# A hybrid decoder layer on Trainium2: gated-unit columns ahead of the decay projection, vectors fetched by another queue

## The chip, the core and the metric

The kernel runs on one core of one Trainium2 chip. The metric is device time in microseconds of one execution. The engines of the core are TensorE (PE: matmuls and transposes, results in PSUM), VectorE (DVE), ScalarE (ACT: activations, some with tables of functions that have to be loaded), GpSimd (POOL) and SyncE (SP, which only issues DMAs here). ScalarE can issue DMAs too, on a queue of its own. Engines wait for each other through semaphores: `then_inc` counts one up when an instruction is done, `wait_ge` holds the engine until a count is reached. A DMA counts 16.

## What is computed

A decoder layer on 256 tokens of width 1024 in float32: RMS norm, one projection that feeds forgetting attention (8 heads) and a gated convolution of width 31, an output projection, a second RMS norm, a top-4-of-32 mixture of experts and a final norm. Cut to the part that the change touches:

```
xn = rmsnorm(h, norm_mix_g);  proj = xn @ w_in
q, k, v, f_logit, glu_in = split(proj);  glu_in = glu_in + b_glu
log_f = log_sigmoid(f_logit + b_f)            # (8 heads, 256)
c = cumsum(log_f)                             # s[t, j] = q_t.k_j * scale + c_t - c_j, causal
a, g = split(glu_in);  u = a * sigmoid(g)     # (256, 512)
y = depthwise_conv(u, w_dw, width 31, causal) + b_dw
conv_o = silu(layernorm(y, ln_g, ln_b))
h = h + concat(att_o, conv_o) @ w_out
h = h + moe(rmsnorm(h, norm_ffn_g))           # 32 experts, 12 MB of weights each
```

## The kernel before

Every engine's program is written out by hand, in order. All big weights stream from HBM into a ring of 22 units of 1 MB in SBUF (`ring`), issued by SyncE: first the pieces of `w_in` and `w_out`, then the experts' weights through L422. On the first lap the ring's places are still in use as pieces and scratch, so SyncE waits for `released_slots` before it writes one: the places of the gated unit's weights for `proj_done` 5, of q for 7, of k for 9, of v for 11, and later ones for scores, for parts of the output projection, and so on. From the second lap on it waits for `units_used`, which TensorE counts.

The first 137 us are the layer before the experts. ScalarE issues two DMAs (decay weights `wf_sb` and `bf_col`, L549, L550), loads a table, and then, for each of the two tiles of 128 tokens, squares and sums x (L553) and takes the root (L562); VectorE does the mean, the reciprocal and the scaling (L801, L803, L823). SyncE issues x (L367), then six small vectors (norm gains, biases, L370 and L372), the taps (L373), then the four quarters of the gated unit's weights (L378). TensorE turns the vectors into columns (L1193, L1195; semaphore `vecs_turned`), ScalarE copies them to `cols`, TensorE transposes the normalised tiles (L1189), VectorE scales them by the gain into `xn_t` (L828) and ScalarE does one of the four groups (L568).

TensorE then runs, in this order: the decay projection into four partial sums (8 matmuls, semaphore `f_done`), the transposes of the taps (L1221), and for each of four blocks of 128 channels the columns `a` (8 matmuls) and `g` (8 matmuls) of the gated unit, with the matmul that adds the four partial sums of the decay (`add_f_parts`) between `a` and `g` of block 0. Then come q and k (two passes each), part of v, the attention scores of groups 0 and 1, more of v, and the channel mean of the convolution's layer norm, for which it waits for `tap_done` (the convolution's channel sum).

ScalarE copies the decay's partial sums (L579) and logits (L587), and takes Exp (L589) and Ln (L591) of them, with VectorE steps between (L834 to L844), and only then goes through the blocks: sigmoid of `g` and a copy of `a` with bias (L597, L599), and, once VectorE has multiplied them (L854, `glu(c)`), taps 0 and 1 (L603, L605). VectorE adds the 29 other taps of each block one by one (L875, `tap_done`), into two accumulators by turns, with the next block's product in the middle, and at block 3, five taps before its end, the row maximum of score group 0 (`row_max(0)`, L862), which waits for `scores_done`. L1163 is the line of the helper that all matmuls share.

## Time and profile before

| | us |
|---|---|
| three timed runs | 1044.59, 1046.27, 1046.94 (median 1046.27) |
| profiled execution, its own time | 1044.2 |
| its span, first to last instruction | 1042.5 |
| PE busy in the span | 998.9 (96%) |
| DVE busy | 238.1 (23%) |
| ACT busy | 145.3 (14%) |
| mean granted TensorE clock | 0.990 |
| DMA, all queues | 421.75 MB, mean 405 GB/s |

The profile's page cuts the span into 40 equal slices of 26 us and gives what the DMA engines moved in each:

```profile
GB/s 310 393 414 194 220 367 395 425 416 427 426 427 436 428 430 427 434 426 432 428 435 428 431 429 431 432 429 429 435 426 431 428 432 429 429 433 424 426 425 167
```

The fourth and fifth slices, 78 to 130 us, are the low ones. In the rows further down a time is the start from the span's beginning, and "idle before <-releaser" is how long the engine had stood still and what let it go on. A TensorE matmul in float32 shows as two records, so 8 matmuls are x16.

### The profile page before, as it was taken

What the parts mean: (1) busy time and instruction counts of PE and PEld (TensorE: products, weight loads), DVE (VectorE), ACT (ScalarE), POOL (GpSimd) and SP (SyncE); (2) the same over time, 40 slices, a digit from 0 to 9 for tenths busy, and PEclk for the clock granted to TensorE, in tenths of its full rate; (3) what the DMA queues carried; (4) which work ended last, traced back from release to release, by engine and by line L of the source; (5) the groups of instructions that cost most, each with busy time, mean ns of one, the idle gap of its engine ahead of it and who ended that gap; (6) DMA issues with size and microseconds to landing.
All of it is one profiled execution on the core that took longest, in us unless ns stands there. A gap on an engine that the chain in (4) does not pass through costs nothing.

```text
span 1042.5 us, 12861 instructions
## 1 busy us (share of the span) xinstructions
PE 998.9 (96%) x5770; PEld 410.4 (39%) x5771; DVE 238.1 (23%) x532; ACT 145.3 (14%) x276; POOL 18.6 (2%) x29
## 2 busy tenths in 40 slices
PE   8999999999999999999999999989999999899996
PEld 7875534333333333333333333323333333323332
DVE  3995341111011111111111111101111111101121
ACT  5144320100010101010101001000101001000103
POOL 4000000000000000000000000000000000000001
PEclk9999999999999999999999999999999999999999
DMA  9995699999999999999999999999999999999994
GB/s 310 393 414 194 220 367 395 425 416 427 426 427 436 428 430 427 434 426 432 428 435 428 431 429 431 432 429 429 435 426 431 428 432 429 429 433 424 426 425 167
DMA packets 33381, 421.75 MB, mean 405 GB/s; under 512 B 4031, under 2 KB 8427, under 8 KB 14380
## 3 DMA queue, kind: packets, MB, share of 16 engines
q1 hardware_dynamic: 31772, 420.57, 96.0%
q8 instruction: 47, 0.77, 0.3%
q10 hardware_dynamic: 1552, 0.33, 0.2%
q14 instruction: 10, 0.08, 0.0%
HBM read 419.82 MB, written 1.05 MB: 404 GB/s over the span
## 4 chain that ended last, share of the span: by engine, by line
PE 61%; DMA 36%; DVE 1%; issue 1%; SPq 0%; ACT 0%; POOLq 0%; POOL 0%; DVEq 0%
PE work L1163 52%; DMA ring<-in_w_gu 32%; PE resid L1163 7%; DMA ring<-in_w_down 4%; PE work L1507 1%; DMA ring<-in_norm_ffn_g 0%; PE work L1279 0%; PE work L1470 0%; POOLq L148 0%; DVE main L929 0%; SPq L370 0%; POOL main L543 0%; PE work L1189 0%; DVE main L969 0%; DVE ring L828 0%
## 5 line engine op out<-in xcount | busy, mean ns | idle before, releaser
L1163 PE MATMUL work<-ring,main 128*64 128x512 f32 (+1 forms) x3080 | 684.8, 598 | 28.2 <-DMA ring<-in_w_gu 25.6
L1163 PEld LDWEIGHTS work<-ring,main 128*64 128x64 f32 (+1 forms) x3080 | 223.1, 139 | 471.3 <-issue 429.9
L1065 DVE TENSOR_SCALAR main<-work 128x512 f32<-128x512 f32 x32 | 22.1, 691 | 584.4 <-PE work L1163 584.4
L726 ACT ACTIVATE main<-main 128x512 f32<-128x512 f32 x32 | 20.2, 630 | 460.7 <-DVE main L1065 460.7
L1163 PE MATMUL work<-ring 128*128 128x256 f32 (+2 forms) x308 | 71.9, 403 | 1.8 <-DVE ring L828 0.9
L1163 PE MATMUL resid<-main 128*128 128x512 f32 x128 | 68.2, 618 | 0.9 <-DVE main L1134 0.9
L1163 PE MATMUL work<-bgu_rows,ident 128*64 128x512 f32 x256 | 62.2, 605 | 0.0
L1163 PEld LDWEIGHTS work<-ring 128*128 128x128 f32 (+1 forms) x308 | 55.7, 186 | 16.3 <-issue 8.3
L1163 PEld LDWEIGHTS work<-select,main 128*128 128x128 bf16 x1536 | 46.6, 98 | 26.2 <-issue 25.2
L740 ACT ACTIVATE main<-work 64x512 f32<-64x512 f32 x63 | 37.2, 591 | 117.9 <-PE work L1163 117.2
L1163 PE MATMUL work<-select,main 128*128 128x64 bf16 x1536 | 50.5, 194 | 0.1
L1058 DVE TENSOR_SCALAR lent<-count,place,gates 128x64 f32<-128x64 f32 x64 | 16.8, 306 | 146.9 <-PE work L1470 139.1
L875 DVE SCALAR_TENSOR_TENSOR main<-ring,main 128x256 f32<-128x256 f32 x116 | 46.6, 478 | 1.3 <-ACT main L605 1.2
L731 ACT ACTIVATE main<-work 128x512 f32<-128x512 f32 x32 | 19.1, 597 | 115.1 <-PE work L1507 115.1
L1072 DVE SCALAR_TENSOR_TENSOR main<-main 128x512 f32<-128x512 f32 x32 | 34.1, 1065 | 1.1
L1163 PEld LDWEIGHTS resid<-main 128*128 128x128 f32 x128 | 19.4, 190 | 27.4 <-issue 27.4
L1163 PE MATMUL resid<-ring,main 128*128 128x512 f32 (+1 forms) x68 | 28.8, 572 | 0.0
L1069 DVE TENSOR_TENSOR main<-main 128x512 f32<-128x512 f32 x32 | 22.2, 692 | 5.4 <-ACT main L726 5.4
L1163 PEld LDWEIGHTS work<-bgu_rows,ident 128*64 128x64 f32 x256 | 15.4, 135 | 19.4 <-issue 17.7
L1507 PEld LDWEIGHTS work<-ident,main 128*128 128x128 f32 x128 | 15.8, 141 | 17.9 <-issue 17.0
L737 ACT ACTIVATE main<-work 128x256 f32<-128x256 f32 x16 | 6.1, 383 | 114.7 <-PE work L1470 114.7
L1066 DVE TENSOR_SCALAR main<-work 128x512 f32<-128x512 f32 x32 | 21.8, 680 | 0.0
(188 smaller groups left out, 275.1 us busy)
## 6 DMA issues: line engine op xcount, KB each, us to landing
ring<-in_w_gu SPq DMA_DIRECT2D x36, 4096.0 KB, 41.6
ring<-in_w_gu SPq DMA_DIRECT2D x36, 2048.0 KB, 16.6
ring<-in_w_down SPq DMA_DIRECT2D x18, 4096.0 KB, 43.8
ring<-in_w_gu SPq DMA_DIRECT2D x8, 3072.0 KB, 37.5
ring<-in_w_down SPq DMA_DIRECT2D x11, 2048.0 KB, 15.6
ring<-in_w_down SPq DMA_DIRECT2D x20, 1024.0 KB, 14.2
ring<-in_w_gu SPq DMA_DIRECT2D x15, 1024.0 KB, 27.2
ring<-in_w_down SPq DMA_DIRECT2D x4, 3072.0 KB, 40.2
```

Of the source, the lines that this page charges most:

```text
L726: nc.scalar.activation(sig_h, gate_h, ACT.Sigmoid, scale=SWIGLU_ALPHA).then_inc(sig_ready, 1)
L731: nc.scalar.activation(to, work[:, act_bank(n), :], ACT.Copy).then_inc(act_t_ready, 1)
L737: nc.scalar.activation(scatter_sb[buffer][0:rows, :], work[0:rows, TURN_BANK, 0:TB * P], ACT.Copy).then_inc(scatter_ready, 1)
L740: return nc.scalar.activation(y_sb[buffer][h][parity * CAP:(parity + 1) * CAP, :], work[h * CAP:(h + 1) * CAP, bank, :], ACT.Copy)
L875: V.scalar_tensor_tensor(acc, u_pad[:, c, j:j + SEQ], dw_cols[:, c, j:j + 1], acc, ALU.mult, ALU.add)\
L1058: done = V.tensor_scalar(weighted[:, t, parity * CAP:(parity + 1) * CAP], count[:, bass.ds(r * CAP, CAP)], place[:, t, bass.ds(e, 1)], gat ...
L1065: V.tensor_scalar(gate_h, work[:, GATE_BANK, :], SWIGLU_LIMIT, None, ALU.min).then_inc(gate_clamped, 1)
L1066: V.tensor_scalar(up_h, work[:, UP_BANK, :], SWIGLU_LIMIT, -SWIGLU_LIMIT, ALU.min, ALU.max).then_inc(up_clamped, 1)
L1069: V.tensor_tensor(sig_h, sig_h, gate_h, ALU.mult).then_inc(glu_ready, 1)
L1072: V.scalar_tensor_tensor(gate_h.rearrange("p (b j) -> p j b", b=4), up_h.rearrange("p (j b) -> p j b", b=4), 1.0, sig_h.rearrange("p (j b) ...
L1163: return nc.tensor.matmul(out_, lhsT, rhs, start=start, stop=stop, skip_group_check=True)
L1507: last = nc.tensor.transpose(work[:, act_bank(n), j * P:(j + 1) * P], gate_h[:, j * P:(j + 1) * P], ident[:, :])
```

## The change

Four things are changed.

- The six small vectors are issued by ScalarE at the very start of its program, not by SyncE; the decay weights and `bf_col` are issued by ScalarE later, behind its copies of the transposed tile.
- ScalarE copies `cols` between the square and the root of the second tile, not behind both.
- TensorE's order is: transposes of the taps, columns of blocks 0 and 1, decay projection, `a` of block 2, the matmul that adds the decay's parts, `g` of block 2, then block 3 behind a wait for ScalarE's copy of the decay logits.
- ScalarE does block 0's activations first and the decay's Exp and Ln between the blocks; VectorE does the decay steps between the taps of block 1, at taps 5, 11 and 17, and the next block's product at tap 23 in blocks 0 and 1 (at 15 in block 2, as before).

```diff
@@ SyncE
             for t in range(TB):
                 sp.dma_start(x_sb[:, t, :], x[0, t * P:(t + 1) * P, :]).then_inc(x_in[t], 16)
-            at = 0
-            for vec, n in ((norm_mix_g, KB), (b_glu, 2 * CB), (b_dw, CB), (ln_g, CB), (ln_b, CB)):
-                sp.dma_start(vec_rows[at:at + n, :], vec.rearrange("(a p) -> a p", p=P)).then_inc(vecs_in, 16)
-                at += n
-            sp.dma_start(gain_rows, norm_ffn_g.rearrange("(m q) -> m q", q=4 * P)).then_inc(vecs_in, 16)
             sp.dma_start(dw_rows, w_dw).then_inc(dw_in, 16)
@@ ScalarE
-            act.wait_ge(wf_zeroed, 1)
-            act.dma_start(wf_sb[:, :, 0:HEADS], ...).then_inc(wf_in, 16)
-            act.dma_start(bf_col[:, :], ...).then_inc(bf_in, 16)
+            at = 0
+            for vec, n in ((norm_mix_g, KB), (b_glu, 2 * CB), (b_dw, CB), (ln_g, CB), (ln_b, CB)):
+                act.dma_start(vec_rows[at:at + n, :], vec.rearrange("(a p) -> a p", p=P)).then_inc(vecs_in, 16)
+                at += n
+            act.dma_start(gain_rows, norm_ffn_g.rearrange("(m q) -> m q", q=4 * P)).then_inc(vecs_in, 16)
...
                 mean_square(x_sb[:, t, :], xn[:, t, :], stat[:, t:t + 1], x_squared)
+                if t == TB - 1:
+                    act.wait_ge(vecs_turned, 1)
+                    nc.scalar.activation(cols[:, :], work[:, 3, 0:36], ACT.Copy).then_inc(cols_ready, 1)
                 act.wait_ge(x_mean, t + 1)
                 nc.scalar.activation(stat[:, 4 + t:5 + t], stat[:, 2 + t:3 + t], ACT.Sqrt).then_inc(x_root, 1)
-            act.wait_ge(vecs_turned, 1)
-            nc.scalar.activation(cols[:, :], work[:, 3, 0:36], ACT.Copy).then_inc(cols_ready, 1)
...
             done.then_inc(xnt_acted, 1)
+            act.wait_ge(wf_zeroed, 1)
+            act.dma_start(wf_sb[:, :, 0:HEADS], ...).then_inc(wf_in, 16)
+            act.dma_start(bf_col[:, :], ...).then_inc(bf_in, 16)
...
+            glu_halves(0)
+            first_taps(0)
+            glu_halves(1)
+            act.wait_ge(f_done, 1)
+            nc.scalar.activation(f_parts, work[:, 0, 0:SEQ], ACT.Copy).then_inc(f_copied, 1)
+            first_taps(1)
+            act.wait_ge(proj_done, F_SUM_DONE)
             act.wait_ge(bf_in, 16)
             nc.scalar.activation(fg[:, 0, :], work[0:HEADS, 0, 0:SEQ], ACT.Identity, bias=bf_col[:, :]).then_inc(proj_copied, 1)
             act.wait_ge(fg_step, 1)
             nc.scalar.activation(fg[:, 2, :], fg[:, 1, :], ACT.Exp).then_inc(decay_exp, 1)
             act.wait_ge(fg_step, 2)
             nc.scalar.activation(fg[:, 4, :], fg[:, 3, :], ACT.Ln).then_inc(decay_exp, 1)
+            for c in range(2, CB):
+                glu_halves(c)
+                first_taps(c)
@@ VectorE
+            NEXT_GLU = (TAPS - 8, TAPS - 8, TAPS // 2, None)
...
-                    if j == TAPS // 2 and c + 1 < CB:
+                    if j == NEXT_GLU[c]:
                         glu(c + 1)
+                    if (c, j) == (1, 5):
+                        decay_below()
+                    if (c, j) == (1, 11):
+                        decay_plus_one()
+                    if (c, j) == (1, 17):
+                        decay_sums()
                     if (c, j) == (CB - 1, TAPS - 6):
                         row_max(0)
@@ TensorE
+            for c in range(2):
+                glu_columns(c, "glu_a")
+                glu_columns(c, "glu_g").then_inc(proj_done, 1)
             pe.wait_ge(wf_in, 16)
             for kb in range(KB):
                 i = kb % 4
                 last = mm(work[32 * i:32 * i + 32, 0, 0:SEQ], wf_sb[:, kb, :], xn_t[:, kb, :], kb < 4, kb >= 4)
             last.then_inc(f_done, 1)
...
+            pe.wait_ge(cols_ready, 2)
+            glu_columns(2, "glu_a")
+            pe.wait_ge(f_sum_ready, 1)
+            pe.wait_ge(f_copied, 1)
+            mm(work[0:HEADS, 0, 0:SEQ], f_sum[:, :], f_parts, True, True).then_inc(proj_done, 1)
+            glu_columns(2, "glu_g").then_inc(proj_done, 1)
+            pe.wait_ge(proj_copied, F_SUM_DONE)
+            glu_columns(3, "glu_a")
+            glu_columns(3, "glu_g").then_inc(proj_done, 1)
```

What stands at three places before and after. First TensorE, from the transposes of the normalised tiles (128x128 x16) to the score matmuls; `32x256` is the decay projection, `128x31` the taps, `128x256` the columns, `8x256` the matmul that adds the decay's parts. Before:

```order
L1189 MATMUL work<-ident,ring 128x128 x16
L1163 MATMUL work<-ring 32x256 x8
L1221 MATMUL work<-ident,ring 128x31 x4
L1163 MATMUL work<-ring 128x256 x8
L1163 MATMUL work<-ring,lent 8x256
L1163 MATMUL work<-ring 128x256 x120
```

and after:

```order
L1209 MATMUL work<-ident,ring 128x128 x16
L1236 MATMUL work<-ident,ring 128x31 x4
L1183 MATMUL work<-ring 128x256 x32
L1183 MATMUL work<-ring 32x256 x8
L1183 MATMUL work<-ring 128x256 x8
L1183 MATMUL work<-ring,lent 8x256
L1183 MATMUL work<-ring 128x256 x88
```

The decay projection has moved behind 32 column matmuls and the adding matmul behind 40; the number of matmuls is the same.

Second ScalarE, from its first instruction to the root of the second tile (`DMA` is an issue). Before:

```order
L549 DMA ring<-in_w_in 128x8x8
L550 DMA bf_col<-in_b_f 8x1
L557 ACT_TABLE_LOAD
L557 ACTIVATE stat<-ident 128x1
L553 ACTIVATE ring,stat<-main 128x1024
L562 ACTIVATE stat<-stat 128x1
L553 ACTIVATE ring,stat<-main 128x1024
L562 ACTIVATE stat<-stat 128x1
L564 ACTIVATE cols<-work 128x36
```

and after:

```order
L546 DMA ring<-in_norm_mix_g 8x128
L546 DMA ring<-in_b_glu 8x128
L546 DMA ring<-in_b_dw 4x128
L546 DMA ring<-in_ln_g 4x128
L546 DMA ring<-in_ln_b 4x128
L548 DMA ring<-in_norm_ffn_g 2x512
L555 ACT_TABLE_LOAD
L555 ACTIVATE stat<-ident 128x1
L551 ACTIVATE ring,stat<-main 128x1024
L563 ACTIVATE stat<-stat 128x1
L551 ACTIVATE ring,stat<-main 128x1024
L561 ACTIVATE cols<-work 128x36
```

Six issues stand ahead of the table load where two stood, and the copy of `cols` stands ahead of the second root.

Third VectorE, in block 1 of the convolution (`128x256` of L875 or L889 is one tap, `8x256` a decay step). Before, the seven decay steps stood ahead of the first product:

```order
L834 SCALAR_TENSOR_TENSOR ring<-ring 8x256
L836 TENSOR_SCALAR ring<-ring 8x256
L838 SCALAR_TENSOR_TENSOR ring<-ring 8x256
L839 MEMSET ring 8x256
L841 SCALAR_TENSOR_TENSOR ring<-ring 8x256
L843 TENSOR_SCALAR ring<-ring 8x256
L844 TENSOR_SCALAR ring<-ring 8x256
L848 MEMSET ring 128x256
L854 TENSOR_TENSOR ring<-ring,main 128x256
```

and after, they stand between taps of block 1:

```order
L889 SCALAR_TENSOR_TENSOR main<-ring,main 128x256 x4
L845 SCALAR_TENSOR_TENSOR ring<-ring 8x256
L889 SCALAR_TENSOR_TENSOR main<-ring,main 128x256 x6
L849 TENSOR_SCALAR ring<-ring 8x256
L889 SCALAR_TENSOR_TENSOR main<-ring,main 128x256 x6
L853 SCALAR_TENSOR_TENSOR ring<-ring 8x256
L854 MEMSET ring 8x256
L856 SCALAR_TENSOR_TENSOR ring<-ring 8x256
L858 TENSOR_SCALAR ring<-ring 8x256
L859 TENSOR_SCALAR ring<-ring 8x256
L889 SCALAR_TENSOR_TENSOR main<-ring,main 128x256 x6
```

None is added or taken away; each of the three groups waits for ScalarE with taps queued behind it.

## Rows read from the trace of the kernel before

**Rows 1.** Stages: from:to, us, busy PE, PEld, DVE, ACT, POOL, PEclk, DMA share, GB/s

```profile
76.00:87.00 11.00, 10.95 (x31) 5.58 (x32) 8.46 (x15) 7.48 (x17) 0.00 (x0) 1.00 0.16 67
...
165.00:510.00 345.00, 343.79 (x2074) 128.34 (x2071) 56.08 (x113) 32.81 (x57) 0.00 (x0) 1.00 1.01 428
```

**Rows 2.** Timeline, SyncE's weight issues between 60 and 90 us: start, duration, what

```profile
68.31 0.33 SPq L422 DMA_DIRECT2D ring<-in_w_gu  x1
...
86.62 3.12 SPq L422 DMA_DIRECT2D ring<-in_w_gu  x2
```

**Rows 3.** Chain of waits that ended last, its first 76 us: start, us, what

```profile
3.47 3.59 DMA ring<-in_norm_ffn_g
...
10.64 1.07 PE work L1163 x16
...
12.07 63.16 PE work L1163 x292
75.23 0.82 issue
```

**Rows 4.** Timeline, SyncE's issues at the start

```profile
0.77 0.87 SPq L367 DMA_DIRECT2D main<-in_x  x2
1.69 0.37 SPq L370 DMA_DIRECT2D ring<-in_norm_mix_g  x1
...
3.76 0.25 SPq L373 DMA_DIRECT2D ring<-in_w_dw  x1
...
8.80 3.36 SPq L378 DMA_DIRECT2D ring<-in_w_in  x1
```

**Rows 5.** The two DMAs of x, from issue to landing

```profile
DMA to landing us min/median/max: 3.6/4.1/4.6
```

**Rows 6.** Timeline of ScalarE: start, us, what; ACTq is its DMA issue

```profile
1.79 0.44 ACTq L549 DMA_DIRECT2D ring<-in_w_in  x1
2.27 0.73 ACTq L550 DMA_DIRECT2D bf_col<-in_b_f  x1
3.03 1.28 ACT L557 ACT_TABLE_LOAD   x1 [2.90 <-issue]
...
4.44 1.06 ACT L553 ACTIVATE ring<-main 128x1024 f32<-128x1024 f32 x1
...
9.09 0.40 ACTq L574 DMA_DIRECT2D lent<-in_w_router  x1
...
21.55 0.47 ACT L597 ACTIVATE main<-work,cols 128x256 f32<-128x256 f32 x1
...
55.86 0.77 ACTq L609 DMA_DIRECT2D main<-ring  x1
...
56.66 0.64 ACTq L610 DMA_DIRECT2D ring<-ring  x1
```

**Rows 7.** Timeline of VectorE, 7 to 30 us

```profile
8.50 2.08 DVE L828 TENSOR_TENSOR ring<-work,cols 128x512 f32<-128x512 f32 x3
...
18.55 0.28 DVE L836 TENSOR_SCALAR ring<-ring 8x256 f32<-8x256 f32 x1 [1.31 <-ACT ring L589]
20.27 0.41 DVE L838 SCALAR_TENSOR_TENSOR ring<-ring 8x256 f32<-8x256 f32 x1 [1.45 <-ACT ring L591]
...
21.91 0.27 DVE L844 TENSOR_SCALAR ring<-ring 8x256 f32<-8x256 f32 x1
...
22.50 0.42 DVE L854 TENSOR_TENSOR ring<-ring,main 128x256 f32<-128x256 f32 x1
24.07 5.63 DVE L875 SCALAR_TENSOR_TENSOR main<-ring,main 128x256 f32<-128x256 f32 x14 [1.15 <-ACT main L605]
```

**Rows 8.** Timelines of TensorE and VectorE, 70 to 76 us

```profile
71.91 0.22 PE L1163 MATMUL work<-lent 128*128 128x128 bf16 x1
...
72.17 0.69 DVE L862 TENSOR_REDUCE lent<-work 128x4 f32<-128x512 f32 x1
...
75.52 0.42 DVE L885 TENSOR_TENSOR ring<-ring,main 128x256 f32<-128x256 f32 x1
```

More of the change, by code:

```diff
@@ L316, in hybrid_layer @@
         last_half_ready = sem("last_half_ready")
+        GLU_DONE, F_SUM_DONE = (1, 2, 4, 5), 3
         FIRST = 2
@@ L570, in _ @@
             done.then_inc(xnt_acted, 1)
+            act.wait_ge(wf_zeroed, 1)
+            act.dma_start(wf_sb[:, :, 0:HEADS], w_in[:, F_COL:F_COL + HEADS].rearrange("(k p) n -> p k n", p=P)).then_inc(wf_in, 16)
+            act.dma_start(bf_col[:, :], b_f.rearrange("(a b) -> a b", b=1)).then_inc(bf_in, 16)
             act.wait_ge(resid_opened, 1)
@@ L575, in _ @@
             act.dma_start(br_row[:, :], b_router.partition_broadcast(P)).then_inc(router_in, 16)
-            act.wait_ge(f_done, 1)
-            nc.scalar.activation(f_parts, work[:, 0, 0:SEQ], ACT.Copy).then_inc(f_copied, 1)
             act.wait_ge(taps_turned, 1)
@@ L583, in _, with glu_halves, first_taps @@
                                  ACT.Copy).then_inc(cols_ready, 1)
-            act.wait_ge(proj_done, 1)
+            act.wait_ge(cols_ready, 2)
+            act.wait_ge(pads_ready, 1)
+            def glu_halves(c):
+                act.wait_ge(proj_done, GLU_DONE[c])
+                nc.scalar.activation(conv_y[:, c, :], work[:, (1 + c) % 4, SEQ:2 * SEQ], ACT.Sigmoid,
+                                     bias=cols[:, B_G + c:B_G + c + 1])
+                nc.scalar.activation(u_pad[:, c, PAD:PAD + SEQ], work[:, (1 + c) % 4, 0:SEQ], ACT.Identity,
+                                     bias=cols[:, B_A + c:B_A + c + 1]).then_inc(proj_copied, 1)
+            def first_taps(c):
+                act.wait_ge(u_ready, c + 1)
+                nc.scalar.activation(conv_y[:, c, :], u_pad[:, c, 0:SEQ], ACT.Identity, scale=dw_cols[:, c, 0:1],
+                                     bias=cols[:, B_DW + c:B_DW + c + 1]).then_inc(taps_started, 1)
+                nc.scalar.activation(conv_odd[:, c, :], u_pad[:, c, 1:1 + SEQ], ACT.Copy, scale=dw_cols[:, c, 1:2]).then_inc(taps_started, 1)
+            glu_halves(0)
[5 more added lines that the diff above has]
+            act.wait_ge(proj_done, F_SUM_DONE)
             act.wait_ge(bf_in, 16)
@@ L1213, in _, with glu_columns @@
             pe.wait_ge(xnt_acted, 1)
+            pe.wait_ge(dw_in, 16)
+            for c in range(CB):
+                last = nc.tensor.transpose(work[:, 3, 32 * c:32 * c + TAPS], dw_rows[:, c * P:(c + 1) * P], ident[0:TAPS, 0:TAPS])
+            last.then_inc(taps_turned, 1)
+            def glu_columns(c, name):
+                if c % 2 == 0:
+                    pe.wait_ge(glu_in[c // 2][name], 16)
+                return columns(BANK_OF[2 + c], 0 if name == "glu_a" else SEQ, name, c)
+            for c in range(2):
+                glu_columns(c, "glu_a")
+                glu_columns(c, "glu_g").then_inc(proj_done, 1)
             pe.wait_ge(wf_in, 16)
```

63 lines of the change are left out of this document (16 added, 47 removed).

## The prediction

> **What bounds the kernel now.** I read the busy times by stage first. From 165 us the sixteen DMA engines run at a share of 1.01 and move 428 GB/s, and the page's slices stay between 413 and 436 until the last one, while between 76 and 87 us they move 67 GB/s [rows 1]. So most of the span is a weight stream at its full rate, and what can move the end is how long that stream stood still before. It stood still because it had nowhere to write: the SyncE queue issues its next weights at 68.31 and only then at 86.62 us [rows 2], and the list of releases in the code ties these to the projections k and v being finished by TensorE. Up to about 137 us every release is an event of TensorE's program, so a shift of TensorE's program between 76 and 137 us is a shift of the end by the same amount, and bytes that arrive sooner before 76 us buy nothing.
>
> The chain of waits then shows what sets TensorE's program [rows 3]. It begins with the small vectors landing at 7.06 us, passes through VectorE to 10.64, and from 12.07 TensorE works 63.16 us without a gap. The one gap is 0.82 us at 75.23, where it waits for the convolution's channel sum. There are therefore two handles on the end: when TensorE's columns start (10.64), and this 0.82 us.
>
> **The 0.82 us wait.** The convolution's taps fill VectorE from 24.07 [rows 7] to 75.94, so an earlier start looks like a gain. But five taps before its end VectorE takes the row maximum of score group 0, at 72.17, and TensorE finishes that group with the fourth causal-mask matmul, 71.91 + 0.22 = 72.13 [rows 8]. VectorE's last tap ahead of it leaves the engine at the same moment. From scores to channel sum it is then a fixed 3.8 us (75.52 + 0.42 − 72.13), and TensorE has 3.1 us of its own work in it (to 75.23). A convolution that arrives sooner waits there for the scores, so the 0.82 us stays. I count 0 for it; were the row maximum no gate, it would be −0.8.
>
> **The change part by part.**
>
> *Columns first on TensorE.* The same matmuls in another order: 1.07 us of decay projection [rows 3] and the matmul that sums its parts (two of 292 records in 63.16 us, 0.4) move behind the columns. TensorE has no gap, so the sum of its work is the same: 0. New waits on it: the fetch of the decay weights now starts at about 9.5 us, landing 5 us later, needed at 25: hidden. The wait before block 3 for ScalarE's copy of the decay logits: that copy stands behind the first taps of block 1, which need VectorE's product of block 1. A block is 32 records of 0.216 us, 6.9 us, so TensorE asks at 12.07 + 3 × 6.9 + 0.4 = 33.2, as before. VectorE gives the product of block 1 after 22 of block 0's taps: with the taps' start of 20.9 from below and 0.40 for a tap [rows 7], 20.9 + 8.8 + 0.4 = 30.1. From product to both first taps is 1.15 (22.92 to 24.07 [rows 7]), the copy 0.5: 31.8. Covered by 1.4 us. If that cover went, q, k and everything behind would slip by the excess.
>
> *Convolution sooner, decay steps inside it.* Block 0's columns ended at 12.07 + 6.9 + 0.4 = 19.4 and ScalarE, busy with the decay, took them at 21.55 [rows 6]. Now they end at 19.4 − 1.07 − 0.4 = 17.9, with up to 0.5 for the pipeline behind the last matmul 18.4. The taps, 2.52 us behind the sigmoid, start at 20.9, 3.15 earlier. VectorE's seven decay instructions then stand between taps: 0.41 (like that at 20.27) + 0.28, and for the other five from 20.27 to 21.91 + 0.27 = 22.18, in all 2.6 us [rows 7]. Net VectorE reaches the row maximum 0.5 us earlier than before, measured against TensorE's start. That is inside the wait for the scores, so 0, and the cover is 0.5 us. ScalarE has six taps (2.4 us) for one table load (1.28 [rows 6]) and one activation of about 0.4 between two of these steps: hidden with 0.7 over. There is one table load more than before, for the sigmoid of block 2: it needs some 2.6 us behind the second step (0.45 + 1.28 + 0.85), VectorE asks 6.7 us behind it (twelve taps and 1.9): hidden.
>
> *Vectors from ScalarE's queue: the start.* What it removes: TensorE no longer waits until 7.06 for the vectors. But VectorE is next: its three scaled copies start at 8.50, when the second normalised tile is ready, and fill it for 2.08 us [rows 7]. Only the gap inside them goes: −0.1 us. The second tile comes from ScalarE: table load at 3.03, first square at 4.44, then a strict ladder of square, mean, root, reciprocal for two tiles [rows 6]. The load starts the moment ScalarE has issued its two DMAs (2.27 + 0.73 = 3.00). x's own landing, 3.6 us after its issue at 0.77, gives 4.37 [rows 4, 5], so this ladder can gain 0.07 us at most from a faster ScalarE.
>
> What it adds: six issues on ScalarE ahead of that table load, instead of two behind a GpSimd wait. Price of one: on SyncE the six took 3.76 − 1.69 = 2.07 us, 0.345 each with the gaps, and a small one 0.25 [rows 4]; ScalarE's own issues took 0.44, 0.73, 0.40 and, for the decay rows later, 0.77 and 0.64 [rows 6]. From 0.77 on: at 0.25 and 0.04 of gap they end at 2.5 (a gain, cut to 0.07 by x); at 0.77 they end at 5.6, 2.6 us later than now. I take 0.46, close to ScalarE's three issues of the first 10 us (median 0.44, mean 0.52): 0.77 + 6 × 0.50 = 3.8, so the table load slips by 0.75 us and with it squares, roots and the second tile. Start of the columns: +0.75 − 0.1 = +0.65 us.
>
> One new wait: ScalarE copies the vector columns between square and root of tile 1, and the root, then VectorE's reciprocal, are queued behind. It costs nothing if the vectors are turned when the square ends, before 7.8 by this count. They are issued by 3.8 and behind less data than before, when the last took 3.6 us [rows 3]: by 7.4 at the latest, then 0.7 on TensorE: 0 to 0.3, taken as 0.
>
> *Weights on SyncE 2.07 us sooner* (1.69 to 3.76 [rows 4]): they run into the same releases: 0.
>
> Sum: 0 + 0 + 0.65 + 0 = +0.65 us. Against the profiled execution (1044.2 us, span 1042.5) that is 1044.85. The three timed runs have their median 2.1 above it, so for a median: 1046.27 + 0.65 = 1046.9.
>
> **A page against the change.** ScalarE's issue of 0.40 us at 9.09 [rows 6] lies wholly inside a SyncE issue of 3.36 us [rows 4], so here one queue did not hold the other. The Trainium skill ("Perfetto Trace Analysis", section "DMA Instruction — HWDGE (DVE, Sync)") says that the descriptor generator is locked for one sequencer at a time. By that rule the issues of x and of the taps (0.87 + 0.25 [rows 4]) would be added to ScalarE's six, 1.1 us: the columns would start 1.75 us later, and the median would be 1048.0. The trace speaks against it; its chance is within that of rival 1.
>
> **Rivals.**
> 1. *ScalarE pays the high price for small shapes (slower).* Its three issues with fewer than 16 rows took 0.73, 0.77 and 0.64 us; two of 128 rows 0.44 and 0.40 [rows 6]. The vectors have 8, 4 and 2 rows. At 0.7 the issues end at 5.2, the table load slips by 2.2, the columns by 2.1; at 0.77 by 2.5. Time 1048.4 to 1048.8. It decides the sign of the verdict from 0.7 per issue on. Against: SyncE's small ones were its cheapest [rows 4]. Chance 0.22.
> 2. *The wait goes (faster, small).* If VectorE's own work and not the scores held the row maximum, 0.5 to 0.8 of the 0.82 us goes: −0.8 − 0.1 with cheap issues, 1045.4. Chance 0.09.
> 3. *The stream's head start counts.* If the 2.07 us carried through to the end: 1044.2. Against: 11 us of nearly idle DMA right behind. The Trainium skill ("DMA: Bandwidth & Descriptors", section "Issuing engines are not separate DMA queues") says that issuing from several engines saves only the sequencer's time; that is this 2.07 us. Chance 0.04.
> 4. *Vectors late.* They land after 8 us, ScalarE stands on the copy with the root behind: 1 to 3 us, 1047.5 to 1049.5. Chance 0.05.
> 5. *Decay steps cost more than their 0.5 us of cover:* each microsecond beyond it is one on TensorE at 75 us. About 1047.5. Chance 0.04.
> 6. *The forecast*, start between −0.1 and +1.4: chance 0.56.
>
> **Numbers.** 1046.9 us. Low end: rival 2 and half of what the three runs of before lie under their median (1.7): 1044.5. High end: rival 1's 1048.8: 1048.9. Two runs differ by up to 0.2% (1044.59 to 1046.94), so about 0.2%, 2.1 us, is what can be told from no change. Faster by more: rival 3 and a share of rival 2 through scatter, 0.09. Slower by more: two thirds of rival 1, half of 4, and some scatter of the forecast, 0.21. Same: 0.70.
>
> **What would show it.** In the profile after: ScalarE's six issues, their lengths and the start of its first table load (3.8); the first column matmul near 11.3; first taps near 21.6; VectorE idle before the row maximum of group 0, waiting for TensorE; the gap on TensorE before the channel mean still about 0.8; the issue that was at 86.62 moved by the same as the columns. The prediction is wrong if the gap before the mean is gone, if TensorE waits anywhere between its columns and the scores, or if the end moves by another amount than that SyncE issue.

## The result and the profile after

The changed kernel took 1047.82 us (median of 12 runs, 1046.51 to 1051.91), the kernel before 1045.01 us beside it (12 runs, 1043.99 to 1046.94). The ratio is 1.0025, with a 95% interval of [1.0018, 1.0033]: slower by 2.6 us (1.9 to 3.4). The same kernel, timed again in another series, gave 1.0018 [1.0008, 1.0027].

The execution that was profiled is the longest of the twelve (1051.91 us). Its profile has a long stretch at the lower clock, told further down. The main reading is from a second profile of the same kernel, label `after_again`, own time 1046.21 us, span 1044.4 us. That is the shortest of its eleven runs, and the profile of before (1044.2 us) is near the short end too.

Its chain of waits begins like this (start, us, what), and answers to [rows 3]:

```profile
2.80 5.42 DMA ring<-in_norm_ffn_g
8.26 0.24 PE work L1213
...
8.99 0.20 ACT cols L561
...
9.52 0.77 DVE ring L833
10.33 0.67 PE work L1209 x4
11.02 1.30 DVE ring L838 x2
12.37 0.43 PE work L1236 x4
12.79 7.12 PE work L1183 x32
20.00 1.28 ACT L589
21.29 0.47 ACT main L589
...
22.23 0.44 DVE ring L867
...
23.81 8.46 DVE main L889 x22
```

Before, the chain went from TensorE's 63 us of matmuls straight to the channel mean. Now it passes ScalarE's copy of `cols` (L561) and the second root behind it (L563), leaves TensorE after block 0's columns (12.79 to 19.91), takes a table load of 1.28 us on ScalarE, and then stays on VectorE's taps (L889) all the way. Two things are late: the start of TensorE's program (12.37 instead of 10.64 us, +1.73), and VectorE's end.

VectorE in block 1, where the seven decay steps now stand, and at the end of the convolution (timeline of VectorE, same kernel):

```profile
38.26 0.41 DVE L845 SCALAR_TENSOR_TENSOR ring<-ring 8x256 f32<-8x256 f32 x1
...
40.97 0.27 DVE L849 TENSOR_SCALAR ring<-ring 8x256 f32<-8x256 f32 x1
...
43.55 0.41 DVE L853 SCALAR_TENSOR_TENSOR ring<-ring 8x256 f32<-8x256 f32 x1
...
45.18 0.27 DVE L859 TENSOR_SCALAR ring<-ring 8x256 f32<-8x256 f32 x1
...
74.25 0.68 DVE L875 TENSOR_REDUCE lent<-work 128x4 f32<-128x512 f32 x1
...
77.61 0.42 DVE L905 TENSOR_TENSOR ring<-ring,main 128x256 f32<-128x256 f32 x1
```

and the channel mean on TensorE, which answers to the 0.82 us of [rows 3]:

```profile
78.13 2.39 PE L1183 MATMUL work<-ring 128*128 128x256 f32 x6 [1.01 <-DVE ring L905]
```

The row maximum of score group 0 (L875) starts without any idle time ahead of it: VectorE does not wait for the scores, it is itself late. From first tap to channel sum VectorE took 78.03 − 23.81 = 54.22 us, before 75.94 − 24.07 = 51.87: 2.35 us more, the decay steps. Its first tap is only 0.26 us earlier than before. So its end is 2.09 us later. TensorE alone would have been ready at 78.13 − 1.01 = 77.12, before at 75.23: 1.89 later. The mean starts at 78.13 instead of 76.05, +2.08 us, and the next things follow by the same amount: the first SyncE issue behind the stalled weights, `spare<-in_w_down`, starts at 91.87 instead of 89.79.

```profile
91.87 0.43 SPq L422 DMA_DIRECT2D spare<-in_w_down  x1
```

Both timed series, +2.6 us (1.9 to 3.4) and +1.9 us (0.8 to 2.8), contain these 2.08 us, and the spans of the two profiles differ by 1.9. That the weight stream behind this point hands the shift on to the end as it is, is an inference that fits these figures.

### The profile page after: what moved, and what is told of

It reads as the page before. It is cut to its first block, busy times and chain, and to the rows that moved or that the text cites. A ratio compares the mean times of both kernels' runs of the same rounds, so it can differ in the third digit from the quotient of the medians.

```text
span 1050.2 us, 12862 instructions
## 1 busy us (share of the span) xinstructions
PE 1007.9 (96%) x5770; PEld 414.6 (39%) x5771; DVE 238.0 (23%) x532; ACT 146.7 (14%) x277; POOL 18.6 (2%) x29
## 4 chain that ended last, share of the span: by engine, by line
PE 60%; DMA 31%; DVE 6%; issue 1%; ACT 0%; ACTq 0%; POOLq 0%; POOL 0%; SPq 0%; DVEq 0%
PE work L1183 51%; DMA ring<-in_w_gu 31%; PE resid L1183 7%; DVE main L889 4%; PE work L1527 1%; DMA ring<-in_norm_ffn_g 1%; PE work L1209 0%; PE work L1490 0%; PE work L1299 0%; ACTq L546 0%; DVE main L902 0%; DVE ring L905 0%; DVE ring L867 0%; POOLq L148 0%; DVE main L949 0%
## 5 line engine op out<-in xcount | busy, mean ns | idle before, releaser
L1085 DVE TENSOR_SCALAR main<-work 128x512 f32<-128x512 f32 x32 | 22.1, 692 | 585.0 <-PE work L1183 585.0
L1183 PE MATMUL work<-ring 128*128 128x256 f32 (+2 forms) x308 | 75.0, 414 | 1.0 <-DVE ring L905 1.0
L889 DVE SCALAR_TENSOR_TENSOR main<-ring,main 128x256 f32<-128x256 f32 x116 | 46.8, 476 | 1.2 <-ACT main L598 1.1
L741 ACT ACTIVATE main<-work 128x512 f32<-128x512 f32 x32 | 19.1, 597 | 115.1 <-PE work L1527 115.1
L1098 DVE TENSOR_TENSOR main<-work,cols 128x512 f32<-128x512 f32 (+1 forms) x33 | 21.7, 661 | 1.7 <-PE work L1183 1.7
```

What stands on the lines that cost most here:

```text
L741: nc.scalar.activation(to, work[:, act_bank(n), :], ACT.Copy).then_inc(act_t_ready, 1)
L889: V.scalar_tensor_tensor(acc, u_pad[:, c, j:j + SEQ], dw_cols[:, c, j:j + 1], acc, ALU.mult, ALU.add)\
L1085: V.tensor_scalar(gate_h, work[:, GATE_BANK, :], SWIGLU_LIMIT, None, ALU.min).then_inc(gate_clamped, 1)
L1098: V.tensor_tensor(tok_t[:, rows, :], work[:, OUT_BANK, :].rearrange("p (k c) -> p k c", k=KB)[:, rows, :], cols[:, G_FFN + rows.start:G_FF ...
L1183: return nc.tensor.matmul(out_, lhsT, rhs, start=start, stop=stop, skip_group_check=True)
```

## Experiments

All ratios are to the kernel before, timed on the same chip in the same series (three series on three chips; 11 or 12 runs of each kernel, 4 of `start_only`). "First column" and "first tap" are starts in the timelines of TensorE and VectorE (the chain of waits has the first column some 0.05 us later). "Marker" is the start of that SyncE issue in the profiled execution. It shows what the first 90 us of that one execution did, and leaves out the scatter of the rest.

| kernel | ratio, 95% | first column | first tap | wait before mean | marker |
|---|---|---|---|---|---|
| before | 1 | 12.03 | 24.07 | 0.82 | 89.79 |
| after_again | 1.0018 [1.0008, 1.0027] | 12.72 | 23.81 | 1.01 | 91.87 |
| order_only | 1.0018 [1.0009, 1.0028] | 12.64 | 23.80 | 1.01 | 91.86 |
| cols_late | 1.0009 [1.0000, 1.0018] | 12.09 | 23.17 | 1.02 | 91.25 |
| vecs_before_weights | 1.0019 [1.0010, 1.0029] | 12.97 | 25.75 | 1.01 | 93.80 |
| start_only | 1.0091 [1.0076, 1.0107] | 20.39 | – | 0.82 | 99.95 |
| preload | 1.0017 [1.0008, 1.0026] | 13.48 | 23.29 | 0.82 | 92.44 |
| preload_scores | 1.0009 [0.9999, 1.0019] | 13.49 | 23.31 | 0 | 91.39 |
| order_preload_scores | 1.0012 [1.0003, 1.0021] | 12.13 | 22.25 | 0 | 90.34 |
| more_warm | 1.0017 [1.0008, 1.0026] | 12.70 | 23.79 | 1.01 | 91.85 |
| taps_sooner | 1.0001 [0.9992, 1.0010] | 12.62 | 23.16 | 0.82 | 90.37 |
| scores_first | 0.9998 [0.9989, 1.0007] | 12.24 | 24.28 | 0.81 | 89.98 |
| taps_and_scores | 0.9984 [0.9975, 0.9993] | 12.58 | 23.12 | 0 | 89.27 |

Two things limit how finely the markers can be compared. The profile of before is the earliest of its kind: TensorE begins to turn the vectors at 7.10 us in it, and at 7.29 to 7.64 in the five other profiles with the vectors on SyncE's queue. The first weights land 7.9 us behind their issue in it and 8.0 to 8.5 behind it in those five. So a marker difference to before of half a microsecond can be scatter of these landings. And a stretch at the lower clock, told in the section on the clock, is in a marker in full, though not every execution need have it: `vecs_before_weights` has +4.01 us at the marker, its twelve runs say +2.0 (1.0 to 3.0).

### The two halves of the change: queue and order

**after_again**, the changed kernel once more.

> The changed kernel once more, nothing edited. It took 1.0025 of the kernel before, and its one profile (a slow one of its twelve runs, 1051.9 us) shows the vectors landing at 8.28 us instead of 7.06, TensorE idle from 7.0 to 8.3 and then granted half the clock from 9.7 to 19.8 us. Theory A (the late vectors and the half clock behind them are what the change costs): ratio 1.002 to 1.004, vectors again at 8.0 to 8.5 us, and again a stretch at half clock ahead of the columns, perhaps a shorter one in a faster run. Rival B (the decay steps between VectorE's taps and the sigmoid's table load cost it): same ratio, but with the full clock the convolution still ends late.

**order_only**: the changed order, but the vectors on SyncE's queue, the decay weights first on ScalarE's, and the copy of `cols` behind both roots, all as before.

> The new order on TensorE, ScalarE and VectorE, with the vectors issued by SyncE, the decay weights first on ScalarE, and the copy of the columns behind both roots, all as in the kernel before. Theory A: the start is that of the kernel before (columns by 11.0 us, full clock), so the ratio is 1.000 within 0.001, and the gap on TensorE before the channel mean is still 0.8 us. Rival B: ratio 1.002 or more. The third view, that an earlier convolution takes the 0.82 us: ratio 0.9992.

The vectors land at about 7.6 us and the tile is ready at 11.15, 0.5 later than in the profile of before. Yet the first column stands still until its weights are there:

```profile
12.64 17.73 PE L1182 MATMUL work<-ring 128*128 128x256 f32 x91 [1.06 <-DMA ring<-in_w_in]
```

In the kernel before, the same DMA was issued at 4.06 and landed 7.9 us later, at 12.0 (the shortest of the four landings of L378, 7.9/11.8/13.3 us), and the first column started at 12.07. The 1.07 us of decay projection and 0.43 of tap transposes ahead of it had filled exactly this wait. With the projection moved behind, 1.06 us of TensorE are lost and the projection still has to be done.

About half of the 1.06 is this execution's later landing (12.6 us); in `order_preload_scores` the wait is 0.53. A fair pair is `taps_sooner`, with the old order and the first weights as late: its first column is at 12.62, that of `order_only` at 12.64, and the marker is 1.49 us sooner, 90.37 against 91.86. Of that 1.3 us is the projection among the columns (from first column to the end of TensorE's work ahead of the mean 63.20 us there, 64.47 here) and 0.2 the longer wait before the mean.

By the ratio, 1.0018 [1.0009, 1.0028], the order by itself costs as much as the whole change. That is neither the 1.000 of theory A nor quite the 1.002 of rival B, and the columns did not start by 11.0 as theory A had it.

**start_only**: the kernel before with the other half, the queues and the early copy of `cols`, and the old order. The vectors' six issues stand first in ScalarE's program, that of the decay weights behind its four copies of `xn_t`. The diff is shortened; the copy of `cols` moves as in the change.

```diff
-            sp.dma_start(vec_rows[at:at + n, :], ...)
-            act.dma_start(wf_sb[:, :, 0:HEADS], ...)
+            act.dma_start(vec_rows[at:at + n, :], ...)
...
+            act.dma_start(wf_sb[:, :, 0:HEADS], ...)
```

> The kernel before with the first half of the change alone: the six vectors issued by ScalarE at its start, the decay weights and bf_col issued behind its copies of the turned tile, the vector columns copied between square and root of the second tile. The order on TensorE and VectorE is that of before, so the decay projection waits for its weights, which are now issued near 10 us. Theory: the vectors land near 8.2 us and not 7.1, the second tile is ready about 1 us later, xn_t near 11.8, and TensorE then waits for the decay weights until about 15: the end moves by 4 us, ratio 1.004. Rival (the weights land 3.5 us after their issue and the late start is all): ratio 1.002. If moving the vectors cost nothing: 1.001 or less.

It is 9.5 us slower, more than expected. TensorE waits for the decay weights, and they take 8 us, not the 3.5 of the rival or the 5 that the prediction counts (chain of waits, then TensorE's timeline):

```profile
9.81 8.02 DMA ring<-in_w_in
...
17.96 1.93 PE L1164 MATMUL work<-ring 128*32 128x256 f32 x16 [6.92 <-DMA ring<-in_w_in]
19.83 0.63 PE L1222 MATMUL work<-ident,ring 31*128 31x31 f32 x4
20.39 5.52 PE L1164 MATMUL work<-ring 128*128 128x256 f32 x16
```

The same DMA took 4.7 us in the kernel before, issued at 1.79 ahead of the weights, and 8.2 in `after_again`, issued at 10.20: issued while the four gated weights are in flight, it lands much later. And the granted clock is 0.50 from 14 to 24 us, so the projection and block 0's columns run at half speed (the projection 1.93 instead of 1.07 us). The halves do not add up: moving the decay weights' fetch is only harmless because the order moved the projection away.

**cols_late**: the changed kernel with the copy of `cols` behind both roots.

```diff
-                if t == TB - 1:
-                    act.wait_ge(vecs_turned, 1)
-                    nc.scalar.activation(cols[:, :], work[:, 3, 0:36], ACT.Copy).then_inc(cols_ready, 1)
...
+            act.wait_ge(vecs_turned, 1)
+            nc.scalar.activation(cols[:, :], work[:, 3, 0:36], ACT.Copy).then_inc(cols_ready, 1)
```

> The changed kernel with one edit: ScalarE copies the vector columns behind both roots, as before, so that the second root does not stand behind the late vectors. Theory A: the second tile is ready at about 8.6 us instead of 10.3, TensorE transposes from 9.0 to 10.5, VectorE's three copies end at about 11.6, columns 1.5 us earlier than in the changed kernel: ratio 1.001 if the clock stays up, less gained if the half clock remains. If ScalarE's standing on the vectors costs nothing: ratio as the changed kernel, 1.0025.

The second root comes at 7.43 us, not 9.09, and the marker 0.62 us earlier. The ratio is half as far from 1, though its interval overlaps that of `after_again`. So this one wait, which the prediction priced at 0, costs about 0.6 us by the profiles. The 1.5 us of theory A were counted from the slow profile; here both profiles have the full clock. In the changed kernel it reads (ScalarE, `after_again`):

```profile
8.99 0.20 ACT L561 ACTIVATE cols<-work 128x36 f32<-128x36 f32 x1 [1.78 <-PE work L1215]
9.09 0.19 ACT L563 ACTIVATE stat<-stat 128x1 f32<-128x1 f32 x1
```

ScalarE stands 1.78 us with the root behind. What is left of the late start, 11.73 instead of 10.64 for TensorE's first instruction behind the tile, is the vectors' landing: 8.15 instead of 7.06.

**vecs_before_weights**: the changed kernel, with SyncE holding the gated weights back until the vectors are in.

```diff
             sp.dma_start(dw_rows, w_dw).then_inc(dw_in, 16)
+            sp.wait_ge(vecs_in, 96)
```

> The changed kernel with one wait added on SyncE: the first weights are issued only when the six vectors have landed. If the weights that now run ahead of them on the same DMA engines are what delays the vectors (theory A's first half), they land at about 5.5 to 6.0 us, TensorE turns them before its warming matmuls cool, the columns start by 10.7 us at the full clock, and the ratio is 1.000. The first weights start 3 us later and are still in time. If the vectors are late for another reason (ScalarE's queue itself), they land at 8 us again and the ratio is 1.0025 or more.

The vectors land at 7.60 us, between the two answers that were expected. With only x and the taps in flight the last vector still needs 4.78 us from its issue. With the weights in flight it needs 5.04 to 5.49 in the seven profiles with the vectors on ScalarE's queue, and 3.59 to 4.11 in the five that show it on SyncE's. So the weights in flight account for 0.3 to 0.7 us of the lateness, and the larger part, 0.7 to 1.2 us, goes with the issue from ScalarE, beside x's two DMAs and not behind them; whether it is the queue or the neighbours is not settled. The price is that the weights land at 12.93, and the columns run partly at half clock (0.50 at 14 to 16 us).

### The sigmoid's table load

**preload**: one dummy sigmoid ahead of the waits of block 0.

```diff
+            nc.scalar.activation(stat[:, 15:16], ident[:, 0:1], ACT.Sigmoid)
             act.wait_ge(cols_ready, 2)
             act.wait_ge(pads_ready, 1)
```

> The changed kernel with one activation more (a sigmoid of one column whose result nobody reads) ahead of the semaphore waits of block 0, so that the sigmoid's table is loaded while TensorE still works on block 0. Theory (the end is set by VectorE's taps, whose start was held by TensorE's late columns and then by an uncovered table load of 1.28 us): the sigmoid of block 0 starts within 0.1 us of block 0's last column, the taps start 1.28 us sooner (22.5 us instead of 23.8), VectorE arrives at the row maximum of group 0 at 73.1 and waits there until the scores are done at 73.9, the wait of TensorE before the channel mean falls from 1.0 to 0.8 us, and the ratio to the kernel before is 1.0014 (was 1.0018). Rival without a gate at the row maximum: VectorE's 1.28 us come through until TensorE's own work is the last, the wait falls to 0, ratio 1.0007. Rival that the table load is no cause: taps start unchanged, ratio 1.0018.

The load leaves the path: the sigmoid starts 0.1 us behind block 0's last column (20.78), and the first tap 9.8 us behind the first column; in `after_again` that is 11.1. But VectorE then waits at the row maximum, and TensorE's wait stays:

```profile
74.81 0.69 DVE L876 TENSOR_REDUCE lent<-work 128x4 f32<-128x512 f32 x1 [0.99 <-PE work L1184]
...
78.70 1.53 PE L1184 MATMUL work<-ring 128*128 128x256 f32 x4 [0.82 <-DVE ring L906]
```

This is the gate that the prediction named, with its 0.82 us. The table load is a cause of VectorE's lateness, but with it gone the gain ends after 0.2 us at the gate; the ratio does not move measurably. The columns began 0.76 us later than in `after_again` here, because the transposes before them ran at half clock.

### The gate at the row maximum

Three kernels on the base of the kernel before. **taps_sooner** adds the decay's parts six matmuls sooner and loads the sigmoid's table ahead (the diff is shortened):

```diff
                     if (c, name) == (0, "glu_a"):
+                        columns(BANK_OF[2 + c], at, name, c, range(0, 2))
                         add_f_parts()
+                        last = columns(BANK_OF[2 + c], at, name, c, range(2, KB))
@@ ScalarE
             nc.scalar.activation(fg[:, 4, :], fg[:, 3, :], ACT.Ln).then_inc(decay_exp, 1)
+            nc.scalar.activation(stat[:, 15:16], ident[:, 0:1], ACT.Sigmoid)
```

> The kernel before, in its own order, with the matmul that adds the decay's parts six matmuls sooner and the same dummy sigmoid behind the decay's Ln, so that the taps start about 2 us sooner (22.0 instead of 24.07 us) while TensorE's start and work are the same. It tests the statement of the prediction that a convolution that comes sooner waits at the row maximum of group 0 for the scores. Theory: VectorE stands idle about 2 us ahead of the row maximum (until 72.1 us), the wait of TensorE before the channel mean stays 0.8 us, ratio 1.0000. Rival (VectorE's own work holds the wait): the wait is gone, ratio 0.9992.

**scores_first** only moves the scores of group 0 on TensorE:

```diff
-            values(10, range(0, 3))
             pe.wait_ge(decay_in, 32)
             pe.wait_ge(proj_copied, 8)
             scores(0)
+            values(10, range(0, 3))
```

> The kernel before with only the scores of group 0 moved ahead of the first three blocks of v on TensorE; taps start as before (24.07 us). Theory: VectorE came to the row maximum at the very moment at which the scores were done, so the opened gate alone gives nothing: the wait before the channel mean stays 0.8 us, ratio 1.0000; together with the taps_and_scores run this says that both parts are needed for the gain. Rival (the scores alone were the limit): wait gone, ratio 0.9992 or less.

**taps_and_scores** does both.

> The same as taps_sooner, and on TensorE the scores of group 0 stand ahead of the first three blocks of v, not behind them, so they are done 1.7 us or more sooner. Theory: the gate opens, VectorE's earlier taps come through, the wait before the channel mean falls from 0.8 us to 0.1 or less, the weight issue that was at 86.62 us moves to about 85.8, ratio 0.9992. Rival (something else holds the wait, or the end does not follow it): ratio 1.0000. If the score matmuls now wait for ScalarE's copies of k: slower by that wait.

VectorE at the row maximum and TensorE at the mean in `taps_sooner`, then VectorE behind the mean in `taps_and_scores`:

```profile
72.75 0.69 DVE L863 TENSOR_REDUCE lent<-work 128x4 f32<-128x512 f32 x1 [1.42 <-PE work L1164]
...
76.64 3.67 PE L1164 MATMUL work<-ring 128*128 128x256 f32 x9 [0.82 <-DVE ring L886]
```

```profile
76.24 1.22 DVE L891 TENSOR_TENSOR main<-main,work 128x1024 f32<-128x1024 f32 x1 [0.46 <-PE work L1164]
```

The taps of `taps_sooner` began at 23.16 us and not at 22.0: TensorE's columns began 0.6 us later than in the profile of before, and the sigmoid then had to wait for them, not for the decay. So only part of the 2 us that were expected reached the gate. Taps that begin sooner wait 1.42 us at the row maximum and win nothing (1.0001). Scores that are done sooner win nothing either (0.9998), because VectorE arrives at that moment anyway. Both together remove the wait: now VectorE waits for TensorE. The marker is at 89.27 although this execution's program began 0.43 us later than that of before (11.07 against 10.64), so 0.95 us net, against 0.82 expected; against `taps_sooner`, whose program began at 11.06, it is 1.10. The ratio, 0.9984 [0.9975, 0.9993], says −1.7 us (−0.7 to −2.6) and contains that. This kernel beats both the one before and the changed one.

### What is left when the waits are mended

**preload_scores** is the changed kernel with the copy behind the roots, the dummy sigmoid and the early scores. **order_preload_scores** is the same, with the vectors and decay weights on the queues of before.

> The changed kernel mended at three places: the copy of the vector columns behind both roots, the dummy sigmoid ahead of block 0's waits, and the scores of group 0 ahead of the first blocks of v. Theory: columns start near 12.2 us as in the run with the copy behind the roots, taps start near 21.9, VectorE has its channel sum at 76.2 and TensorE comes to the channel mean at 76.4, no wait there; 0.4 us later than in the kernel before, ratio 1.0004. What is left is the later start of the columns, 1.1 us against the prediction's 11.3 less. Rival (the queue or the clock costs something besides): ratio 1.001 or more.

> The changed order on TensorE, ScalarE and VectorE, but the vectors on SyncE's queue as before, the decay weights first on ScalarE's, the table of the sigmoid loaded ahead of the waits, and the scores of group 0 ahead of v. Nothing of the vectors' lateness, of the uncovered table load or of the gate is left. Theory: the first columns now stand where the decay projection stood and wait for the landing of the first gated unit's weights, near 12.6 us; the decay projection no longer fills that time, so TensorE's work ends 0.8 us later than in the kernel before: ratio 1.0007 to 1.0009, no wait before the mean. Rival (the weights' landing is no limit, columns start at 11.3): ratio 0.9995.

In neither does TensorE wait before the mean. The second still loses: its tile was ready at 11.18 and its first column waited for the weights,

```profile
11.18 0.43 PE L1236 MATMUL work<-ident,ring 31*128 31x31 f32 x4 [0.94 <-DVE ring L838]
12.13 14.18 PE L1183 MATMUL work<-ring 128*128 128x256 f32 x63 [0.53 <-DMA ring<-in_w_in]
```

and with the projection now behind it, the marker is 0.55 us later than before, and 1.07 later than in `taps_and_scores`, which has the same mends and the old order. That this equals the 1.07 us of the decay projection is chance: the first column is 0.45 us sooner (12.13 against 12.58), and the way from there to the marker 1.52 us longer. Some 1.2 of it is the projection among the columns, as in `after_again`; the other 0.3 is a second wait for weights, in front of `g` of block 0, where TensorE's weight load stands 0.45 us for the next quarter, until 15.89. In the old order the projection covers that one too.

The ratio of `order_preload_scores`, 1.0012, is a little more than the expected 1.0007 to 1.0009, with these inside its interval. `preload_scores` came late at the start: its first column is at 13.49 and not near 12.2, because the 16 transposes ahead of it ran at half clock (3.54 us). Its ratio, 1.0009 [0.9999, 1.0019], fits the expected 1.0004 and the rival's 1.001 alike.

### The clock

**more_warm**: the changed kernel with 14 instead of 10 matmuls in the stretch that fills TensorE until the vectors land.

> The changed kernel with 14 matmuls in place of 10 in the stretch that keeps TensorE busy until the vectors land. In four of the six profiles with the vectors on ScalarE's queue the granted clock fell to half behind this wait (1.6 us and more of idle time) and the 16 tile transposes took 3.4 to 3.5 us, not 2.0. Theory (the idle time leads to the fall): TensorE is idle 0.5 us ahead of the vectors, the clock is full from 7 to 14 us, columns start near 12.8 us, and the ratio is 1.0015 or somewhat less (was 1.0018 and 1.0025). Rival (the fall has another cause): half clock in 8 to 12 us as before, columns at 13.5, ratio 1.002.

The expectation says that the four profiles at half clock had 1.6 us and more of idle time and slow transposes. Three had the slow transposes, behind 1.32, 1.57 and 1.62 us; the fourth, `vecs_before_weights`, had 0.42 us there, full clock in the transposes, and half clock only in the columns.

In `more_warm` TensorE's idle time ahead of the vectors fell from 2.11 to 0.81 us and the granted clock was 1.00 from 8 to 20 us. The ratio, 1.0017, is that of `after_again`. One profile at full clock does not show that the idle time was the cause, since `after_again` and `cols_late` had full clock with 2.1 us of it; and the ratio did not move. What makes the clock fall stays open.

A share of it in the 2.6 us can't be excluded: of the eight profiles with the vectors on ScalarE's queue five have a stretch at half clock ahead of 25 us, of the six with them on SyncE's none. It is not needed for the loss, though: `order_only` has no such stretch and the same ratio as `after_again`.

## Why the prediction was right or wrong

The time fell into the range (1047.82 in 1044.5 to 1048.9), the likeliest verdict did not hold: same was given 0.70, slower by over 0.2% 0.21, and it was slower, by 0.25% (0.18 to 0.33) in the first series and 0.18% (0.08 to 0.27) in the second. How close 1047.82 is to the forecast's 1046.9 is in part luck. The forecast added its 0.65 us to the median of three runs, 1046.27, and the median of twelve is 1045.01; from there it would have said 1045.7. The change cost 2.6 us and not 0.65. The upper end of the range came from rival 1, which did not happen; the time that was measured was made by what rival 4 describes. Point by point:

- **What bounds the kernel.** Right. The marker moved by what TensorE's program moved at the mean: +2.08 and +2.08 in `after_again`, +1.46 and +1.46 in `cols_late`, and the ratios of both contain these. One figure of the reading is off: the lowest of the page's slices from 182 us on is 416, not 413, and nothing hangs on it.
- **The 0.82 us wait.** Right for the kernel before, and shown by `taps_sooner` and `preload`: 1.42 and 0.99 us of VectorE's idle time at the gate, 0.82 left before the mean. The text took the gate for the only case, though. It holds as long as VectorE comes early; in the changed kernel VectorE came late and the wait was 1.01.
- **Issue price on ScalarE** (0.46 us each, 0.75 us of slip). Wrong, too dear. The six issues ended at 3.18 us and the table load slipped 0.18 us. Rival 1 falls:

```profile
0.77 0.59 ACTq L546 DMA_DIRECT2D ring<-in_norm_mix_g  x1
1.40 0.29 ACTq L546 DMA_DIRECT2D ring<-in_b_glu  x1
...
2.80 0.38 ACTq L548 DMA_DIRECT2D ring<-in_norm_ffn_g  x1
3.21 1.28 ACT L555 ACT_TABLE_LOAD   x1 [3.08 <-issue]
```

- **"They are issued by 3.8 and behind less data than before … by 7.4 at the latest."** This is the step that failed and weighs most at the start. They were issued 0.67 us sooner and landed 1.16 us later, at 8.22: 5.42 us from issue, not 3.6. The 3.6 us of SyncE's vectors were carried over to another queue. Part of the 1.16 is that the profile of before is an early one; between the medians of the profiles on either queue it is about 0.7. With that the new wait of ScalarE, counted at 0, stood 1.78 us. This was rival 4, given 0.05. The start was +1.73, of which 1.09 is the landing (`cols_late`) and 0.64 the copy; the forecast's +0.65 was counted for a slip of the table load that was 0.18, so that it equals the copy's part is chance.
- **"TensorE has no gap, so the sum of its work is the same: 0."** The sum is nearly (from first column to the end of TensorE's work ahead of the mean 64.40 us, before 63.20 and the projection's 1.07, together 64.27), but the projection was also the cover for the landing of the first weights. The text looked for gaps in the trace of before and found none; it did not ask what the moved work had covered. In the changed kernel the late vectors hide this: weights issued at 2.06 land at 11.7 (9.6 us, the shortest of four), only 0.3 sooner than before for an issue 2.0 sooner, and the first column is at 12.79. Had the vectors been on time, with the column free to start at 11.1 us as the profile of before would allow, the weights would have held it up to 11.7. With the vectors back on SyncE's queue and the weights behind them they do hold it, in `order_only` (1.06 us) and `order_preload_scores` (0.53 us).
- **The taps "start at 20.9, 3.15 earlier", later 21.6 with the slip.** Wrong by 2.2 us: 23.81. Block 0 ended at 19.91, not 19.1 (0.9, from the late start). The 0.5 us that the text allowed for the pipeline behind the last matmul had no row behind it; the load that waits for block 0 starts 0.1 us behind it. And the sigmoid's table load was left out. The text took the 2.52 us from sigmoid to first tap, which hold no load, since in the kernel before it had run at 20.26 inside the decay's chain; the one it did count was for block 2. In the changed kernel this load starts only when the columns are done, at 20.00, and costs its full 1.28.

```profile
20.00 1.28 ACT L589 ACT_TABLE_LOAD   x1 [6.64 <-PE work L1183]
```

- **Decay steps, 2.6 us, cover 0.5 us net of the earlier taps.** The price was right (2.35), the cover was not there: −0.26 + 2.35 = +2.09 on VectorE, and TensorE's own 1.89 hides all but 0.19 of it. That is rival 5's mechanism on top of rival 4's. Rival 4 had been given 0.05 and rival 5 0.04, each as if alone; here the late landing and the table load brought both at once.
- **Block 3's wait, the decay fetch, the Exp and Ln between taps.** Hidden, as said: TensorE has no gap from 12.79 to 77.12.
- **The weights 2.07 us sooner: 0.** No run has this alone. They were issued 2.00 us sooner and the first landed 0.3 sooner, and the marker behind the stall moved with TensorE all the same, so nothing of it is seen at the end.
- **The page on the locked descriptor generator** ("Perfetto Trace Analysis" of the Trainium skill, section "DMA Instruction — HWDGE (DVE, Sync)"). ScalarE's six issues ran beside SyncE's issues of x and took 0.29 to 0.59 us, with no 1.1 us more for them. No run here shows a lock at issue time. Whether something like it is behind the late landing can't be told from these traces.

## What to carry to other kernels

When work is moved away from in front of something, ask what it had covered: a landing DMA directly behind it shows no gap in the trace of before, and its landing time has to be compared with the new start. A DMA's time from issue to landing, read in one place of the program, need not hold in another: here 3.6 to 4.1 us behind x on SyncE's queue became 5.0 to 5.5 beside x on ScalarE's, and 4.7 us for the decay weights became 8. And an event that two engines reach at the same moment has to be moved on both, as the two halves of `taps_and_scores` show, each worth nothing alone.

## What was not expected of the hardware

- Six small vectors issued by ScalarE between 0.77 and 3.2 us landed 5.42 us behind the start of the last issue; issued by SyncE, behind x, 3.59 us behind it (up to 4.11 in other profiles). Without the weights in flight it was still 4.78.
- A DMA of 8 columns of the decay weights, issued by ScalarE at 9.81 behind four 1 MB transfers, landed 8.02 us later; issued at 1.79 ahead of them it had taken 4.7.
- The sigmoid's table load stood behind the semaphore waits that precede its activation in the program: ScalarE was idle for 6.64 us ahead of it in `after_again`. An activation of one element ahead of the waits moved it: in `order_preload_scores` it ran at 12.67 us, seven us before its sigmoid.
- In the longest run's profile of the changed kernel the granted clock was 0.50 between 10 and 19 us, the lower of the two levels (1.2 GHz), behind 1.32 us in which TensorE stood still for the vectors. The 16 transposes of the tile took 3.35 us, not 2.0, and block 0's columns 10.09, not 7.12:

```profile
9.03 3.35 PE work L1209 x16
...
13.78 10.09 PE work L1183 x32
23.96 1.28 ACT L589
```

There the marker is at 95.84 us, 4.0 us behind `after_again`. `preload` and `preload_scores` show the half clock too, up to 12 us only, after 1.6 us of idle time, `start_only` from 14 to 24 us, in and after its 6.92 us, and `vecs_before_weights` at 14 to 16 us, behind a wait of 0.79 us. `after_again` and `cols_late` had 2.1 us of idle time and kept the full clock. So the clock can be halved for up to ten microseconds near the start, and the length of the idle stretch just ahead of it does not tell whether it will be.
